# A hybrid attention, recurrence and expert layer: every 128x128 transposition outside attention made as two 64-row ones

## What is computed

```
u   = rms(x, norm1_g)
q, k, v, x_lru, g_lru = split(u @ w_in)               # 1024 -> 5 * 512
a   = stick_breaking(q, k, v)                         # 8 heads of 64
r   = rglru(conv4(x_lru)) * gelu(g_lru)               # 8 blocks of 64
h   = x + concat(rms(a, sb_norm_g), rms(r, lru_norm_g)) @ w_out
u2  = rms(h, norm2_g)
y   = rms(h + moe(u2), final_g)                       # 4 groups of 8 experts, top 1 group, top 2 experts
```

## Time and profile before

| | us |
|---|---|
| median of 3 runs (lowest, highest) | 4329.56 (4327.42, 4331.07) |
| the profiled execution, its own time | 4338.74 |
| its span, first to last instruction | 4337.0 |
| PE busy in it | 4111.1 |
| DVE, ACT, POOL busy in it | 2823.5, 2488.2, 688.2 |

### The profile page before, as it was taken

One profiled execution on the slowest core, in us unless ns is written; L12 is line 12 of the kernel. 1 busy time (PEld: TensorE's weight loads), 2 busy tenths in 40 slices (PEclk: granted clock), 3 DMA queues, 4 the chain that ended last, 5 costly groups with the idle time before them and its releaser, 6 DMA issues. The chain is left out here.

```text
span 4337.0 us, 83225 instructions
## 1 busy us (share of the span) xinstructions
PE 4111.1 (95%) x27983; PEld 3112.2 (72%) x27985; DVE 2823.5 (65%) x3211; ACT 2488.2 (57%) x3370; POOL 688.2 (16%) x916
## 2 busy tenths in 40 slices
PE   8999989997999999999998999869999999999997
PEld 6888867774555555555555888758888888888886
DVE  3222235668998998999996555476666655555665
ACT  4222225557887887887886333246666655545665
POOL 0000002221000000000001111003332333223332
PEclk9999999998999999999999999979999999999999
DMA  5444443313111112111102344247666654555674
GB/s 202 182 144 177 152 173 122 111 68 115 31 32 59 31 31 60 31 31 53 36 7 99 141 155 155 97 169 255 222 243 225 223 204 166 204 195 198 242 262 143
DMA packets 308629, 590.32 MB, mean 136 GB/s; under 512 B 38704, under 2 KB 104240, under 8 KB 308400
## 3 DMA queue, kind: packets, MB, share of 16 engines
q1 hardware_dynamic: 257568, 460.82, 30.2%
q0 software_dynamic: 46224, 118.03, 7.9%
q10 hardware_dynamic: 4608, 8.39, 0.5%
HBM read 427.75 MB, written 209.72 MB: 147 GB/s over the span
## 5 line engine op out<-in xcount | busy, mean ns | idle before, releaser
L1171 DVE TENSOR_TENSOR_SCAN att_R<-att_stay,att_R,att_turn 128x1025 f32<-128x1025 f32 x448 | 1024.7, 2338 | 19.1 <-ACT att_stay L1105 19.0
L1115 ACT ACTIVATE att_RT<-att_rt 128x1024 f32<-128x1024 f32 (+1 forms) x576 | 550.4, 956 | 241.4 <-PE att_rt L1053 205.6
L1053 PEld LDWEIGHTS att_rt<-ident,att_R 64*128 64x128 f32 x8448 | 320.2, 139 | 369.5 <-issue 369.3
L1105 ACT ACTIVATE att_stay<-att_z 128x1024 f32<-128x1024 f32 (+2 forms) x576 | 546.6, 949 | 6.0 <-PE att_z L1039 5.6
L1068 PE MATMUL att_out<-att_RT,att_dv 128*64 128x512 f32 (+3 forms) x2304 | 523.7, 576 | 0.0
L1053 PE MATMUL att_rt<-ident,att_R 64*128 64x64 f32 x8448 | 388.0, 228 | 79.2 <-ACT att_RT L1115 65.0
L1619 DVE TENSOR_TENSOR ew_lo<-ew_raw,ew_hi 128x1024 fp32r<-128x1024 f32 x384 | 443.9, 1218 | 22.1 <-ACT ew_hi L1612 13.3
L1612 ACT ACTIVATE ew_hi<-ew_raw 128x1024 fp32r<-128x1024 f32 x384 | 374.0, 1048 | 100.2 <-PE ex_down L2007 93.5
L236 PE MATMUL qkv_out<-u_u_hi,qkv_w_hi 128*128 128x512 f32 x768 | 308.8, 402 | 3.6 <-DVE u_u_lo L227 3.6
L236 PE MATMUL qkv_out<-u_u_hi,qkv_w_lo 128*128 128x512 f32 x768 | 300.6, 391 | 0.0
L236 PE MATMUL qkv_out<-u_u_lo,qkv_w_hi 128*128 128x512 f32 x768 | 300.0, 391 | 0.0
(11 more groups left out here) (282 smaller groups left out, 8303.6 us busy)
## 6 DMA issues: line engine op xcount, KB each, us to landing
ew_raw<-in_w_e_gate SPq DMA_DIRECT2D x32, 2048.0 KB, 9.0
ew_raw<-in_w_e_up SPq DMA_DIRECT2D x32, 2048.0 KB, 9.7
ew_raw<-in_w_e_down SPq DMA_DIRECT2D x32, 2048.0 KB, 9.1
u_x<-in_x SPq DMA_DIRECT2D x32, 512.0 KB, 5.9
s_u_hi<-u_u_hi SPq DMA_DIRECT2D x8, 2048.0 KB, 11.8
s_u_lo<-u_u_lo SPq DMA_DIRECT2D x8, 2048.0 KB, 16.4
mix_x<-in_x SPq DMA_DIRECT2D x32, 512.0 KB, 4.9
s_h<-mix_h SPq DMA_DIRECT2D x32, 512.0 KB, 3.7
```

Of the source, the lines that this page charges most:

```text
L1053: last = nc.tensor.transpose(rt[:, half, qt, h, :], R[lanes, n % 3, qt, h, s * P:(s + 1) * P], k.ident[lanes, lanes])
L1105: done = nc.scalar.activation(stay[:, step % 4, :, 0:width], z_pair[:, :, 0:width], ACT.Sigmoid, scale=-scale)
L1115: nc.scalar.activation(RT[:, s, first:, :, :, :].rearrange("p t h half q -> p (t h) half q"), turned_pair, ACT.Copy).then_inc(rt_copied, 1)
L1171: nc.vector.tensor_tensor_scan(joined(R[:, n % 3, s, :, :]), joined(stay[:, step % 4, :, :]), joined(turn[:, s, :, :]), R[:, (n - 1) % 3, ...
```

## The change

Each 128x128 transposition becomes two, of rows 0 to 63 and rows 64 to 127 of the same block, against the 64x64 corner of the identity that lies on the same partitions. The first writes 64 columns of one PSUM bank, the second 64 columns of another; banks are now chosen by half and not by chunk. The copies that empty the banks put the halves side by side. Since a bank holds one half of two chunks, `qkv` works in pairs of chunks: both are transposed together, both are emptied before the next pair is transposed, and a product of either waits for both. `dv` goes in pairs of `j` as well, later in the group. `norm1_g` moves from the activations to the weights: `high` becomes a plain copy, `low` a plain subtraction, and both `w_in` splits get `gain=k.g_norm1`. The wait ahead of each burst of transpositions is now a `hold`.

```diff
-        self.tr = [ps(f"{tag}tr{i}", [P, GT]) for i in range(2)]
+        self.tr = [ps(f"{tag}tr{i}", [P, 2, TT, HD]) for i in range(2)]
...
         if c == 0:
-            pe.wait_ge(self.x_scaled, G * TT + TT)
-        pe.wait_ge(self.lo_ready, G * DC + c + 1)
-        for t in range(TT):
-            last = nc.tensor.transpose(self.tr[c % 2][:, t * P:(t + 1) * P], self.x[:, t, c * P:(c + 1) * P],
-                                       self.k.ident[:])
-        last.then_inc(self.transposed, 1)
+            hold(pe, self.k, self.x_scaled, G * TT + TT)
+        hold(pe, self.k, self.lo_ready, G * DC + c + 2)
+        for cc in (c, c + 1):
+            for t in range(TT):
+                for half in range(2):
+                    lanes = slice(half * HD, (half + 1) * HD)
+                    last = self.nc.tensor.transpose(self.tr[half][:, cc % 2, t, :],
+                                                    self.x[lanes, t, cc * P:(cc + 1) * P], self.k.ident[lanes, lanes])
+        last.then_inc(self.transposed, 2)
+
+    def half_of(self, rows, n):
+
+
+        return rows[:, n // 2 * 2:n // 2 * 2 + 2, :].rearrange("p c (t half q) -> p half c t q", half=2, q=HD)[:, n % 2]
+
+    def high(self, act, G, steps=range(DC)):
+
+        for n in steps:
+            act.wait_ge(self.transposed, G * DC + n // 2 * 2 + 2)
+            self.nc.scalar.activation(self.half_of(self.hi, n), self.tr[n % 2][:], ACT.Copy).then_inc(self.hi_ready, 1)
+
+    def low(self, dve, G, steps=range(DC)):
+
+        for n in steps:
+            dve.wait_ge(self.hi_ready, G * DC + n + 1)
+            self.nc.vector.tensor_tensor(self.half_of(self.lo, n), self.tr[n % 2][:], f32(self.half_of(self.hi, n)),
+                                         ALU.subtract).then_inc(self.lo_ready, 1)
...
-            pe.wait_ge(self.lo_ready, G * DC + c + 3)
+            pe.wait_ge(self.lo_ready, G * DC + c // 2 * 2 + 4)
...
         for c in range(DC):
+            if c % 2 == 0 and c + 2 < DC:
+                self.transpose(pe, G, c + 2)
             pe.wait_ge(weights.low_ready, c + 1)
...
-            if c + 2 < DC:
-                self.transpose(pe, G, c + 2)
...
 def first_low(dve, weights, ug):
 
-    for c in range(DC):
+    for c in range(0, DC, 2):
         weights.low(dve, [c])
-        ug.low(dve, 0, [c])
+        ug.low(dve, 0, [c, c + 1])
+        weights.low(dve, [c + 1])
...
-        weights = SplitWeights(nc, io.w_in[:, 0:3 * W_SB], 3 * W_SB, sb, sem, "qkv_")
+        weights = SplitWeights(nc, io.w_in[:, 0:3 * W_SB], 3 * W_SB, sb, sem, "qkv_", gain=k.g_norm1)
...
-                    if j > 0:
-                        pe_dv(pe, G, j - 1)
+                    if j == 2:
+                        pe_dv(pe, G, 0)
...
                     if j == 0:
-                        pe_dv(pe, G, NP - 1)
+                        pe_dv(pe, G, 2)
...
         def transpose_x(pe):
-            for half in range(2):
-                for c in range(4):
-                    last = nc.tensor.transpose(x_tr[half][:, c * P:(c + 1) * P],
-                                               xg[:, (4 * half + c) * P:(4 * half + c + 1) * P], k.ident[:])
-                last.then_inc(x_transposed[half], 1)
+            for c in range(DC):
+                for half in range(2):
+                    lanes = slice(half * HD, (half + 1) * HD)
+                    last = nc.tensor.transpose(x_tr[half][:, c * HD:(c + 1) * HD], xg[lanes, c * P:(c + 1) * P],
+                                               k.ident[lanes, lanes])
+                    if c == DC - 1:
+                        last.then_inc(x_transposed[half], 1)
...
         def transpose_hidden(pe, T):
 
-            pe.wait_ge(hidden_ready, T)
-            for half in range(2):
-                for f in range(2 * half, 2 * half + 2):
-                    last = nc.tensor.transpose(h_tr[half][:, (f % 2) * P:(f % 2 + 1) * P], hidden[:, f * P:(f + 1) * P],
-                                               k.ident[:])
-                last.then_inc(h_transposed[half], 1)
+            hold(pe, k, hidden_ready, T)
+            for f in range(FC):
+                for half in range(2):
+                    lanes = slice(half * HD, (half + 1) * HD)
+                    last = nc.tensor.transpose(h_tr[half][:, f * HD:(f + 1) * HD], hidden[lanes, f * P:(f + 1) * P],
+                                               k.ident[lanes, lanes])
+                    if f == FC - 1:
+                        last.then_inc(h_transposed[half], 1)
```

More of the change, by code:

```diff
@@ L308, in first_high @@
 def first_high(act, weights, ug):
-    for c in range(DC):
+    for c in range(0, DC, 2):
         weights.high(act, [c])
-        ug.high(act, 0, [c])
+        ug.high(act, 0, [c, c + 1])
+        weights.high(act, [c + 1])
 def first_low(dve, weights, ug):
-    for c in range(DC):
+    for c in range(0, DC, 2):
         weights.low(dve, [c])
-        ug.low(dve, 0, [c])
+        ug.low(dve, 0, [c, c + 1])
+        weights.low(dve, [c + 1])
 class StoredGroups:
@@ L397, in qkv @@
             out = [ps(f"qkv_out{i}", [P, GT]) for i in range(4)]
-            dv_tr = [ps(f"qkv_dv_tr{i}", [P, GT]) for i in range(2)]
+            dv_tr = ps("qkv_dv_tr", [P, 2, 2, TT, HD])
             st_hi = [sb(f"qkv_st_hi{i}", [P, GT], F32R) for i in range(4)]
@@ L419, in pe_dv @@
             def pe_dv(pe, G, j):
[L420 to L425, removed]
+                hold(pe, k, dv_ready, G * NP + j + 2)
+                hold(pe, k, dv_staged, G * NP + j + 2)
+                for jj in (j, j + 1):
+                    for b in range(TT):
+                        for half in range(2):
+                            lanes = slice(half * HD, (half + 1) * HD)
+                            last = nc.tensor.transpose(dv_tr[:, half, jj % 2, b, :],
+                                                       dv[lanes, jj, b * P:(b + 1) * P], k.ident[lanes, lanes])
+                last.then_inc(dv_transposed, 2)
             def pe_group(pe, G, last, lead=LEAD):
@@ L479, in act_group @@
                     split_high(act, G, m)
[L480 to L481 removed]
+                    if m in (3, 5):
+                        stage_dv(act, G, m - 3)
+                        stage_dv(act, G, m - 2)
                 if not last:
@@ L601, in lru @@
         sb, ps, sem = alloc(nc, outer)
-        weights = SplitWeights(nc, io.w_in[:, 3 * W_SB:], 2 * W_LRU, sb, sem, "lru_", ahead=ahead)
+        weights = SplitWeights(nc, io.w_in[:, 3 * W_SB:], 2 * W_LRU, sb, sem, "lru_", gain=k.g_norm1, ahead=ahead)
         groups.sixth = sb("lru_sixth", [P, 2, GT], F32R, ROW)
@@ L1397, in pe_transposes @@
             def pe_transposes(pe, T, t):
-                pe.wait_ge(u2_ready, T + 2)
-                pe.wait_ge(u2_t_ready, T + 1)
+                hold(pe, k, u2_ready, T + 2)
+                hold(pe, k, u2_t_ready, T + 1)
                 for c in range(DC):
-                    last = nc.tensor.transpose(tr[c // 4][:, (c % 4) * P:(c % 4 + 1) * P], u2[:, t, c * P:(c + 1) * P],
-                                               k.ident[:])
+                    for half in range(2):
+                        lanes = slice(half * HD, (half + 1) * HD)
+                        last = nc.tensor.transpose(tr[half][:, c * HD:(c + 1) * HD], u2[lanes, t, c * P:(c + 1) * P],
+                                                   k.ident[lanes, lanes])
                 last.then_inc(u2_transposed, 1)
@@ L1970, in gate_product @@
             for n, (a, x, w) in enumerate(weights.passes(x_hi, x_lo, 0, range(DC), 0)):
-                if n % 4 == 0 and n < 2 * DC:
-                    pe.wait_ge((x_lo_ready if a is x_lo else x_hi_ready)[n // 4 % 2], T + 1)
+                if n in (0, DC):
+                    for half in range(2):
+                        pe.wait_ge((x_lo_ready if a is x_lo else x_hi_ready)[half], T + 1)
                 if n == 2 * DC:
@@ L2000, in down_product @@
                 for i, (a, h, w) in enumerate(weights.passes(h_hi, h_lo, 2, range(FC), n * GT)):
-                    if n == 0 and i in (0, 2):
-                        pe.wait_ge(h_hi_ready[i // 2], T)
+                    if n == 0 and i == 0:
+                        for half in range(2):
+                            pe.wait_ge(h_hi_ready[half], T)
                     if n == 0 and i == FC:
@@ L2025, in _ @@
                 up_product(pe, e)
-                pe.wait_ge(gathered, T * 16 + 32)
+                hold(pe, k, gathered, T * 16 + 32)
                 transpose_x(pe)
@@ L2057, in hidden_low @@
                 dve.wait_ge(h_hi_ready[half], T)
-                nc.vector.tensor_tensor(h_lo[:, 2 * half:2 * half + 2, :], h_tr[half].rearrange("p (f n) -> p f n", f=2),
-                                        f32(h_hi[:, 2 * half:2 * half + 2, :]), ALU.subtract).then_inc(h_lo_ready, 1)
+                rows = slice(half * HD, (half + 1) * HD)
+                nc.vector.tensor_tensor(h_lo[:, :, rows], h_tr[half].rearrange("p (f n) -> p f n", f=FC),
```

(1 more changed line is left out.)

37 lines of the change are left out of this document (15 added, 22 removed).

## The result

| us | before | changed |
|---|---|---|
| median of 4 runs (lowest, highest) | 4330.32 (4327.42, 4331.96) | 4374.14 (4370.75, 4379.74) |
| span of the profiled execution | 4337.0 | 4378.0 |

The ratio is 1.0094, with a 95% interval of 1.0082 to 1.0106: 44 us slower by the medians, 41 by the ratio (36 to 46), where 8 were forecast. The direction holds, the size doesn't, and the time lies above the range.

The account below looks back on a forecast made before the run. The prediction took TensorE to bound the kernel (busy 4111.1 of 4337.0 us). Burst terms of +7.2 us and +1 at the start made +8.2, carrying the median 4329.56 to 4337.8 us; range 4316 to 4352.

Parts of the forecast that it names:

- What a burst costs now: Last product ahead to second product behind, on TensorE: 1.34 us for 8 whole transpositions, 0.89 for 4.
- what a burst of halves will cost: Same measure, with the array's change of form in and out: 1.30 us for 16 halves, 1.05 for 8.
- the rival of a free change of rows: All halved bursts: a change of rows alone costs nothing, -47 us, 4282 us; chance 0.15.
- `hidden`, +12.8 us: Experts: 80 bursts of 4 transpositions become 8 halves, each 0.16 us dearer; the largest term.
- `x`, -3.2 us: Experts: 81 bursts of 8 transpositions become 16 halves, each 0.04 us cheaper.
- `mix`, -1.3: `mix` stage: 32 bursts of 8 transpositions become 16 halves, each 0.04 us cheaper.
- `u` and `dv`, -1.1 us: Eight groups with bursts joined into 16 halves: `u` in `qkv` gains 0.8 us, `dv` 0.3 us.
- The start, +1: Start of `qkv`: first product 1.6 to 2.2 us late, some regained during weight arrival; booked +1 us, between 0 and 2.2.
- The slower rival: `qkv`, `leading_products`: a pair is emptied too late and TensorE waits; 4348 us, chance 0.17 including any other added wait.
- The step that failed: Experts: 24 products (5.5 us) of `down_product` lie before the halves of `x` are used, so no cost.

Follow-up runs that it names:

- `whole_x`: The changed kernel with `transpose_x` and its copies whole as before, `hold` and late register load kept: 4342.3 us, 1.0017 against the kernel before.
- `early_whole_h`: `early` with `transpose_hidden` and its copies whole as before the change (4 of 128 rows): 4327.6 us, 0.9985 against the kernel before.
- `early`: The changed kernel with the register load of the expert's number moved ahead of `transpose_x`: 4341.7 us, 1.0013 against the kernel before.
- `pairs_whole`: The changed kernel with `u` in `qkv` transposed whole, in the new order of pairs: one execution, 4375.5 us; a `qkv` group took 70.60 us.
- `load_mid`: The changed kernel with the register load put between `transpose_hidden` and `up_product`: 4344.4 us, 1.0021 against the kernel before.
- `loads2`: The kernel before, all transpositions whole, with two more register loads behind `transpose_x`: 4336.0 us, 1.0005.
- `loads4`: The kernel before, all transpositions whole, with four more register loads behind `transpose_x`: 4374.7 us, 1.0092.

## Why the prediction was wrong

By its own steps:

- *What a burst costs now* and *what a burst of halves will cost*: right to 0.01 us by the measure chosen. 1.30 us for 16 halves after, in `mix`, `qkv` and (with the load out of the way) the experts, and 1.05 for 8. The value taken from switches that also change columns was the right one, and the rival of a free change of rows is out; the `hold`, for which the upper bound left a little, costs nothing that shows (`whole_x`). The Trainium skill (page TensorEngine Tiling (Array Packing), section Key Properties) says that changing the tiling mode drains TensorE: the trace agrees in that each such change costs time, for a change of rows alone too, 0.09 us on entering and 0.12 on leaving.
- *`hidden`, +12.8 us*: right, 0.15 us in a tile (17.87 - 17.72), 12 us, by `early_whole_h` against `early`.
- *`x`, -3.2 us; `mix`, -1.3*: `mix` is 0.9 us shorter. `x` halved (`early`) and whole (`whole_x`) can't be told apart, 1.0013 and 1.0017. By the tile, `x` is no gain but 0.01 us of loss, +1 us: the measure ends at the second product, and in the experts the products behind it come late as well (from the first `down_product` to `gate_product` 5.61 us behind halves, 5.55 behind whole ones, medians of `early` and before). That is 4 us that the sum lacks.
- *`u` and `dv`, -1.1 us*: mis-sized, it is some -7 without the start. A steady group went from 71.40 to 70.50 us. I had 0.14 of that; half of the 0.9 is the wait of 0.44 us for the last chunk, which I had not looked for, because I compared bursts and not the products between them. `pairs_whole` keeps it away with whole transpositions (70.60). The joined bursts are worth 0.27 and not 0.14, since a burst of 4 costs 0.444 us in that group and not 0.43, and there are ten; the last 0.2 stays open. The last group, 1.8 us shorter, is in the 7 too; why it is stays open.
- *The start, +1*: the first product starts at 20.18 and not 18.61, 1.6 us late, at the low end of the 1.6 to 2.2 (whose own terms give 1.4 at the lower end); of this nothing came back in the first group (74.9 us against 74.8), so the +1 booked was too little.
- *The slower rival* (a pair emptied too late in `qkv`) did not happen. TensorE's waits for `u_u_lo` in `qkv` shrank from 3.6 us (11 times) to 1.1 (once).
- **The step that failed** is "In the experts both halves of `x` come at the burst's end, but 24 products ... lie before their use. ... No cost." I looked at what the data need, and took the array's start times in attention and `lru` for the price of a burst anywhere. Neither of these places has a register load behind the burst; in the trace before, all of TensorE's are in the experts. Such a load cost nothing before, and I put it at nothing without asking what covered it. Its cover was the sequencer's lead, and the lead goes by the number of instructions. The change halves the work in an instruction and doubles their number: 2.2 us of lead ahead of the burst became none, and of the 1.1 us of register work 0.46 came to light (1.10 - 0.64). A little of it comes back in the products behind, so a tile loses 0.41 us (18.273 - 17.867, changed against `early`): in 80 tiles 32 us, 35 by the times of `early`.

The sum with what the traces show: +8 forecast, +32 for the load, +4 for `x`, -6 for `qkv`, -1 for `hidden`: 37 us. The two profiled executions differ by 41.0, of which 1.7 is attention's; the ratio says 41, from 36 to 46; the medians say 44, with a spread of 9 us among the changed kernel's runs. So 2 us in the traces stay open, and what the medians show above that is inside the spread.

What is shown by runs: that the load's place is the cause (`early`, `load_mid`), that the `hold` by itself isn't (`whole_x`), nor a change of form ahead of 8 halves (`load_mid`), and that the same cost appears with whole transpositions once the register work outlasts the lead (`loads2`, `loads4`). That the lead goes by queue entries and not by time is shown by the same 34 in three mixtures that take from 2.6 to 4.1 us (the table under `load_mid`), and by one forecast that came true. That the sequencer gets no further than the start of a burst of 16 halves is measured but not explained: 34 entries would have let it. A change of form stops it not ahead of 8 halves, but ahead of 16 it isn't ruled out; bursts of 10, 12 or 14 would tell. Not tried were the halves with a plain wait in place of the `hold` ahead of them; `early` shows that with the `hold` the loss goes all the same.

## What to carry to other kernels

In this kernel, splitting matmuls into smaller ones shortened the time by which the sequencer ran ahead: look at what stands behind them on the same queue (a register load here), and put it ahead of the burst or behind a long product. A change of the array's form cost 0.2 us and more for a burst here, in and out, so halves pay only in long bursts: 16 halves broke even, 8 lost 0.15 us, 24 in one place won 0.21 (by the times) to 0.25 (by the tile). Bring all bursts of a loop together before halving them; bringing them together whole gave nothing (17.69 against 17.70 us a tile).

## What was not expected of the hardware

- A load of one number into a register of TensorE's sequencer, with the checks around it, takes 0.76 us (0.65 in a row), 0.3 of it the load itself; with the waits behind it 1.1 us. Two further loads were free under a lead of 2 us; of four, 0.5 us showed (18.21 against 17.70 us a tile).
- When its register load started, the sequencer was 17 matmuls ahead of the array, 34 entries with their weight loads, whether they were products, whole transpositions or 8 halves. Behind 16 halves it didn't come further than the start of the burst.
- Halves kept their pace of 0.03 us each, whether 8, 16 or 24 stood in a row.
